# A stick-breaking triangle as two rounded products, a reordered seam and a later key rotation in a one-core transformer kernel

## The chip, the cores and the metric

The kernel runs on one core of a Trainium2 chip. The metric is the device time of one execution in microseconds (us). Engines are named as the profile names them: PE (TensorE matmul), PEld (TensorE weight load), DVE (VectorE), ACT (ScalarE), POOL (GpSimd) and SP (SyncE, which issues most DMAs).

## What is computed

One transformer block and then a second block of two layers, all in float32, on 256 tokens of width 1024. The part that the change touches most is the stick-breaking attention of the second block's token mixer (8 heads in each of the 2 layers), cut here to what matters:

```python
def stick_breaking_attention(q, k, v):
    ...
        z = jnp.einsum('bhqd,bhkd->bhqk', qc, k).astype(jnp.float32) * scale
        mask = kpos[None, :] < qpos[:, None]
        log_1m = jnp.where(mask, jax.nn.log_sigmoid(-z), 0.0)
        suffix = lax.cumsum(log_1m, axis=3, reverse=True) - log_1m
        w = jnp.where(mask, jnp.exp(jax.nn.log_sigmoid(z) + suffix), 0.0).astype(v.dtype)
        return jnp.einsum('bhqk,bhkd->bhqd', w, v)
```

The token mixer computes 8 heads of causal attention with rotary (moba), these 8 heads (sb) and 8 heads with latent queries and keys (mla), gates their projections and adds the result to x. The first block is built likewise (dilated and neighbourhood attention, then a gated feed-forward with a convolution over positions). Its residual sum has no norm on what is added (`x = x + gate1 * (merged @ w_out)`), while every residual sum of the second block norms it first (`x + res_w * (1 + gate) * rms_norm(y, g_post)`). All scales and shifts come from products of a condition vector with large "ada" matrices.

## The kernel before

**Matmuls.** Weights come in chunks of 128 x 2048 floats, 269 of them. SP loads a chunk into one of three raw buffers, ACT rounds it to float32r (`hi`, L922), DVE writes the remainder (`lo`, L1311, raw minus hi), and PE computes every large product as three float32r products: hi by hi, hi by lo, lo by hi (`three`, L517 to L520). Chunk c is split behind chunk c-3 or c-4, whose slot it takes. A few small products are plain float32: the attention scores (L802), the transposes, the weighted values (L852, L854) and the stick-breaking sums (L813 to L817). A plain float32 matmul is two MATMUL records in the profile.

**Order.** Every engine's instructions are written out by hand in program order, and semaphores join them. In a mixer, step s computes the chunk `slots[s]` on PE, and around it stand the pieces of attention of nearby heads. Heads 0 to 7 are moba (or dil), 8 to 15 are sb, 16 to 23 are mla. Chunks 8 to 15 of the slots are lat.0, lat.1, gate.0, gate.1, gate.2, then `uq`, gate.3 and `ukv` with one latent matrix each; their products are shorter (36 matmuls for uq, 18 for ukv, 48 for a gate).

**A stick-breaking head s** goes over the engines so: PE writes the scores into a PSUM bank (L802). ACT computes ln(1 + exp(-|z|)) into `work` (L1095 to L1099). DVE adds max(z, 0) (L1521, `softplus`) and masks the two diagonal squares (L1524), and raises `s_sp`. One step later PE waits for `s_sp` and adds three products of `work` with constant matrices to the bank (`turned`, L811 to L818): the triangle over the first 128 keys for all 256 queries (L813), ones (L815) and the triangle over the second 128 keys (L817). The chunk of that step stands behind them on PE. DVE then adds the mask (L1528, `log_weights`), and ACT takes exp (L1113).

**DVE in a mixer step**, in order (`mixing`, L1616): copies or merges of the chunk just computed, L1528 of the head before, L1311 of the coming chunk, L1521 and L1524 of this head, extras of the step, `o_second` (L1535), then one or two ada products (L1324, 128 x 1024 each, with their own three buffers and DMAs). The extras of step 12 are the latents: scaled by DVE (L1606), rounded by ACT (L1265), remainder by DVE (L1613), after which PE may start `uq`; and `rotate_mla_k` (L1585 to L1590), which is first read by the scores of head 16. Step 14 has `rotate_mla_q` (L1595 to L1600). At step 16 DVE copies the value parts of ukv out of PSUM (`take_v`, L1569), which frees the bank of gate.4.

**A seam** is where PE has finished a projection by rows (L695) and the next needs the new x: DVE multiplies each of the four PSUM banks by a gain row (`times`, L1438), adds it to x (`plus`, L1453), ACT sums squares and takes the root, x is scaled (`scaled_x`, L1461 and L1465; ACT L984), PE transposes it (L748), with some idle float32 products (`keep_busy`, L738) before and between, and ACT and DVE make `h_hi` and `h_lo`. `into_norm` (L1466) writes the DVE part. Of its un-normed uses only the one behind `o.out` (the tag "out") leads to a norm; the seam behind `o.down` is written out separately (L1741 on).

`ada_places` (L138) is the table that says behind which chunk each ada product stands on DVE; the order of SP's loads follows from it (a load of ada h waits for the use of ada h-3). `shift_and_gain` (L1333) turns finished ada columns into shifts and gains.

Of the kernel before, what the change touches and what calls it, by code (L numbers as in the profile page):

```python
# [12 lines left out]
P = 128  # L13
# [123 lines left out]

def ada_places():  # L138
    at = [-1] * ADA_START
    at += list(range(4, 21)) + [20, 20, 21, 22, 24, 25]  # L140
    at += [AT["o.out.0"] + 2 + i // 2 for i in range(3)]
    b = AT["o.up.0"]
    at += [b + 7 + 2 * i for i in range(6)]
    at += [AT["o.down.0"] + 2 + i for i in (0, 0, 1, 1, 2, 3, 3, 4, 4, 5, 6, 6, 7, 7, 8, FD - 1)]
    for l in range(LAYERS):
        b = AT[f"{l}.up0.0"]
        at += [b + 3 + i for i in range(20)] + [b + 24 + i for i in range(8)]
        s = AT[f"{l}.moba.k1"] + 2
        at += [s + i for i in range(2, 13)] + [s + i for i in range(16, 25)]
        g = AT[f"{l}.up2.0"]  # L150
        at += [g + 3 + i for i in range(8)]
        if l + 1 < LAYERS:
            at += [g + 11 + i for i in range(13)] + [g + 25 + i for i in range(3)]
    return at
# [46 lines left out]
def program(nc, d, known):  # L201

    with ExitStack() as ctx:
# [22 lines left out]
        con = sb("con", [P, NCCOL])  # L226
        dcon = sb("dcon", [P, NDCOL])
        cs = sb("cs", [P, D])
        mod = ada_out
        last_row = dcon[:, 0:D]  # L230
        gain = sb("gain", [P, 2 * 8 + LAYERS * 24])
# [15 lines left out]
        with ExitStack() as scope:  # L247
            sb("br_shift", [P, BR_SHIFT], F32, scope)
            ra = sb("ra", [P, 15, SEQ], F32, scope)
            rb = sb("rb", [P, 12, SEQ], F32, scope)  # L250
            br_hi = sb("br_hi", [P, 12, SEQ], F32R, scope)
            br_lo = sb("br_lo", [P, 12, SEQ], F32R, scope)
            gates_a = sb("gates_a", [P, 12, SEQ], F32, scope)
            with ExitStack() as inner:
                gates_b = sb("gates_b", [P, 8, SEQ], F32, inner)
            lat = sb("lat", [P, 4, SEQ], F32, scope)
            lat_sq = sb("lat_sq", [P, 3, SEQ], F32, scope)
            turn = sb("turn", [P, 2, SEQ], F32, scope)
            turn_qk = gates_a[:, 0:2, :]
            rs, lat_hi, lat_lo = turn, br_hi[:, 8:11, :], br_lo[:, 8:11, :]  # L260
# [253 lines left out]
        def _(eng):  # L514
# [291 lines left out]
            def turned(l, heads, s):  # L806
# [3 lines left out]
                if kind == "sb":  # L810
                    eng.wait_ge(*s_sp.at((l, s)))  # L811
                    bank = score_bank(heads, s)
                    mm(bank[:, 0:SEQ], dcon[:, DCOL["neg_tri"]], w[:, 0:SEQ], start=False, stop=False,  # L813
                       skip_group_check=True)
                    mm(bank[:, P:SEQ], dcon[:, DCOL["neg_ones"]], w[:, SEQ:TRI], start=False, stop=True,  # L815
                       skip_group_check=True)
                    ins = mm(bank[:, SEQ:TRI], dcon[:, DCOL["neg_tri"]], w[:, SEQ:TRI], start=False, stop=True,  # L817
                             skip_group_check=True)  # L818
                else:
                    eng.wait_ge(*s_normed.at((l, s)))  # L820
                    before = [i for i in range(s % 2, s, 2) if heads[i][0] != "sb"]
                    if before:
                        eng.wait_ge(*s_pt_copied.at((l, before[-1])))
                    if kind in ("moba", "mla"):
                        parts = [(0, 0), (P, P), (2 * P, 2 * P)]
                    else:
                        parts = [(u * SEQ + t * P, t * SEQ + u * P) for t in range(2) for u in range(2)]
                    for to, fro in parts:
                        ins = nc.tensor.transpose(turn_bank(s)[:, to:to + P], w[:, fro:fro + P], ident)
# [473 lines left out]
        def _(eng):  # L1303
# [164 lines left out]
            def into_norm(post, banks, pre, buf):  # L1468
# [4 lines left out]
                times(post, banks, buf, 0, 0)  # L1473
                plus(post, buf, 0, normed)
                times(post, banks, buf, 1, 1)
                if pre:
                    scaled_x(pre, buf, 0)
                times(post, banks, buf, 1, 0)
                plus(post, buf, 1, normed)
                if pre:  # L1480
                    half_of_x(pre)
                    scaled_x(pre, buf, 1)
# [34 lines left out]
            def softplus(l, heads, s):  # L1517
# [3 lines left out]
                stt(w[:, 0:TRI], score_bank(heads, s)[:, 0:TRI], 0.0, w[:, 0:TRI], ALU.max, ALU.add)  # L1521
                ve.drain()
                diagonal = two(w[:])[:, :, 0:P]
                tt(diagonal, diagonal, over(dcon[:, DCOL["sb_mul"]], 2), ALU.mult).then_inc(*s_sp.up((l, s)))  # L1524

            def log_weights(l, heads, s):
                eng.wait_ge(*s_turned.at((l, s)))
# [184 lines left out]
            for k in range(3):  # L1712
                if k < 2:
                    split_behind(f"o.out.{k}")
                ada(AT[f"o.out.{k}"])
            shift_and_gain("o.1", 24, par[:, PCOL["b_ada"]][:, 24:40], par[:, PCOL["g_ffn"]], gain[:, 8:16])
            into_norm("out", "o.out", "norm2", oa[:, 0:8, :])
            modulated("norm2", 8)
            split_behind("o.out.2")
# [36 lines left out]
            for l in map(str, range(LAYERS)):  # L1756
# [16 lines left out]
                split_behind(f"{l}.down0.10")  # L1773
                eng.wait_ge(*s_dcon_in.at("dcon"))
                eng.wait_ge(*s_causal_in.at("causal"))
                for i, name in enumerate(("q0", "k0", "v0")):
                    if i < 2:
                        rotate_moba(l, name)
# [1 line left out]
                    ada(AT[f"{l}.moba.{name}"])  # L1780
                mixing(l, MIX_HEADS, "moba.q1", MIX_SLOTS, {
                    0: [lambda: rotate_moba(l, "q1")], 2: [lambda: rotate_moba(l, "k1")], 8: [lambda: layer_post(l, 1)],
                    12: [lambda: latents(l), lambda: latents_second(l), lambda: rotate_mla_k(l)],
                    14: [lambda: rotate_mla_q(l)]})
                split(AT[f"{l}.out.3"])
                layer_gain(l, 2)
# [219 lines left out]
```

## Time and profile before

| what | value |
|---|---|
| median of 3 runs | 1710.9 us (1710.19 to 1712.64) |
| the profiled execution's own time | 1708.62 us |
| its span | 1706.8 us |
| PE busy | 1661.3 us, 97% |
| DVE busy | 1266.4 us, 74% |
| ACT busy | 872.6 us, 51% |
| mean granted TensorE clock | 0.997 |
| DMA | 398.80 MB, mean 234 GB/s |

The profile gives one execution. Busy time of PE is the union of its MATMUL records, which overlap since they are pipelined, so the durations of records add up to more than the busy time; what a matmul costs in a stream is read from the distance of the starts.

### The profile page before, as it was taken

To read this page: it belongs to the slowest core of one execution; us is meant where nothing else is said; L and a number is where in the kernel's file an instruction comes from. 1 tells how busy PE (TensorE), PEld (TensorE's weight loads), DVE (VectorE), ACT (ScalarE), POOL (GpSimd) and SP (SyncE) were. 2 spreads that over 40 slices of the span, in tenths; PEclk is the share of its full clock that TensorE was granted. 3 is DMA by queue.
4 is the path that set the end of the run, shared out by engine and by line. 5 is a ranking of instruction groups with operands and counts; after the bars stand their busy time and mean duration, and the time that the engine had idled before them with its cause. 6 is when DMAs were issued, how large, how long until landed. Compare 5 with 4: busy or idle time off the path is not lost.

```text
span 1706.8 us, 29606 instructions
## 1 busy us (share of the span) xinstructions
PE 1661.3 (97%) x12344; PEld 1551.4 (91%) x12344; DVE 1266.4 (74%) x1852; ACT 872.6 (51%) x1214; POOL 21.7 (1%) x39
## 2 busy tenths in 40 slices
PE   3999999999999999999999999999999999999998
PEld 3999889987999899989989998999899989989997
DVE  7777889977878677776878875877677776878553
ACT  4565466653543365675374344534355676373432
POOL 0000000000000000000000000000000000000000
PEclk9999999999999999999999999999999999999999
DMA  9878756777677745746548786687845746547552
GB/s 376 315 258 248 256 196 227 205 282 291 257 286 275 292 170 181 221 179 231 198 182 294 273 227 262 225 292 277 286 166 189 223 172 233 205 179 259 196 169 93
DMA packets 71078, 398.80 MB, mean 234 GB/s; under 512 B 8224, under 2 KB 8736, under 8 KB 36384
## 3 DMA queue, kind: packets, MB, share of 16 engines
q1 hardware_dynamic: 67968, 387.43, 64.3%
q0 software_dynamic: 2976, 9.47, 1.6%
q8 instruction: 98, 1.61, 0.4%
q14 instruction: 36, 0.29, 0.0%
HBM read 395.79 MB, written 1.08 MB: 233 GB/s over the span
## 4 chain that ended last, share of the span: by engine, by line
PE 76%; DVE 9%; ACT 6%; DMA 4%; DVEq 3%; issue 2%; SPq 1%; ACTq 0%
PE lin L518 17%; PE lin L520 17%; PE lin L519 17%; PE att L695 14%; DVE lo L1311 4%; ACT hi L922 3%; PE att L802 2%; PE lin L558 1%; DMA raw<-in_w 1%; PE lin L560 1%; PE lin L568 1%; DMA ada_w<-in_ada 1%; DVEq L1675 1%; DVE ada_w L1324 1%; ACT work L942 1%
## 5 line engine op out<-in xcount | busy, mean ns | idle before, releaser
L1311 DVE TENSOR_TENSOR lo<-raw,hi 128x2048 fp32r<-128x2048 f32 x269 | 615.4, 2291 | 251.8 <-ACT hi L922 251.5
L518 PE MATMUL lin<-h_hi,hi 128*128 128x256 f32 x2448 | 687.9, 281 | 1.1 <-DVE work L1670 0.7
L520 PE MATMUL lin<-h_hi,lo 128*128 128x256 f32 x2448 | 684.1, 279 | 0.0
L519 PE MATMUL lin<-h_lo,hi 128*128 128x256 f32 x2448 | 683.1, 279 | 0.0
L922 ACT ACTIVATE hi<-raw 128x2048 fp32r<-128x2048 f32 x269 | 513.3, 1911 | 193.2 <-PE att L695 118.3
L518 PEld LDWEIGHTS lin<-h_hi,hi 128*128 128x128 f32 x2448 | 460.4, 188 | 3.8 <-issue 3.7
L519 PEld LDWEIGHTS lin<-h_lo,hi 128*128 128x128 f32 x2448 | 460.5, 188 | 0.1
L520 PEld LDWEIGHTS lin<-h_hi,lo 128*128 128x128 f32 x2448 | 460.2, 188 | 0.0
L1324 DVE CUSTOM_DVE_ANT_0 ada_w<-ada_w,cs 128x1024 f32<-128x1024 f32 x179 | 217.6, 1218 | 18.5 <-DMA ada_w<-in_ada 18.4
L1162 ACT ACTIVATE work<-lin 128x256 f32<-128x256 f32 x88 | 33.8, 384 | 268.5 <-PE lin L520 267.5
L695 PE MATMUL att<-hi,act_hi 128*128 128x512 f32 x440 | 138.8, 389 | 0.0
L695 PE MATMUL att<-hi,act_lo 128*128 128x512 f32 x440 | 138.8, 389 | 0.0
L695 PE MATMUL att<-lo,act_hi 128*128 128x512 f32 x440 | 138.8, 389 | 0.0
L695 PEld LDWEIGHTS att<-lo,act_hi 128*128 128x128 f32 x440 | 82.6, 188 | 17.2
L695 PEld LDWEIGHTS att<-hi,act_lo 128*128 128x128 f32 x440 | 82.6, 188 | 17.2
L695 PEld LDWEIGHTS att<-hi,act_hi 128*128 128x128 f32 x440 | 82.2, 188 | 16.8
L518 PE MATMUL lin<-br_hi,hi 128*128 128x256 f32 x224 | 63.5, 283 | 0.1
L519 PE MATMUL lin<-br_lo,hi 128*128 128x256 f32 x224 | 62.6, 279 | 0.0
L520 PE MATMUL lin<-br_hi,lo 128*128 128x256 f32 x224 | 62.5, 279 | 0.0
L518 PE MATMUL lin<-hi,h_hi 128*128 128x256 f32 x192 | 54.3, 283 | 0.0
L558 PE MATMUL lin<-h_hi,hi 128*128 128x256 f32 x224 | 53.1, 282 | 1.1 <-ACT h_hi L1007 1.1
L520 PE MATMUL lin<-hi,h_lo 128*128 128x256 f32 x192 | 53.9, 281 | 0.0
(291 smaller groups left out, 2024.7 us busy)
## 6 DMA issues: line engine op xcount, KB each, us to landing
raw<-in_w SPq DMA_DIRECT2D x269, 1024.0 KB, 4.9
ada_w<-in_ada SPq DMA_DIRECT2D x179, 512.0 KB, 5.2
ada_s<-in_ada SPq DMA_DIRECT2D x13, 512.0 KB, 15.4
bias<-in_bias POOLq DMA_DIRECT2D x16, 256.0 KB, 4.3
ffn_row<-rows POOLq DMA_DIRECT2D x5, 512.0 KB, 9.2
x<-in_x SPq DMA_DIRECT2D x1, 1024.0 KB, 9.6
ra<-rows POOLq DMA_DIRECT2D x2, 512.0 KB, 5.0
dcon<-in_dcon SPq DMA_DIRECT2D x1, 896.0 KB, 7.6
```

Of the source, the lines that this page charges most:

```text
L518: mm(out, w_hi, a_hi, start=start, stop=False, skip_group_check=skip)
L519: mm(out, w_hi, a_lo, start=False, stop=False, skip_group_check=skip)
L520: return mm(out, w_lo, a_hi, start=False, stop=stop, skip_group_check=skip)
L558: mm(o, hi[SLOT[c]][:, b], h_hi[:, t, :], start=t == 0 and j == 0, stop=False, skip_group_check=True)
L560: mm(o, lo[SLOT[c]][:, b], h_hi[:, t, :], start=False, stop=False, skip_group_check=True)
L568: ins = mm(outs[i][:, j * SEQ:(j + 1) * SEQ], hi[SLOT[c]][:, b], h_lo[:, t, :], start=False, stop=t == 3, skip_group_check=True)
L695: ins = mm(att[:, 2 * a + n, :], act[:, t, tokens], w[s][:, kk * D + n * 512:kk * D + (n + 1) * 512], start=t == 0 and i == 0, stop=t == 2 ...
L802: ins = mm(out, q, k, start=start, stop=stop, skip_group_check=skip)
L922: act(hi[SLOT[c]][:], raw[:, c % RAW, :], ACT.Copy).then_inc(*s_hi.up(c))
L1162: act(work[2 + k % 2][:, 0:SEQ], lin[:, BANK[(c, 0)], 0:SEQ], ACT.Silu).then_inc(*s_gated.up((stage, k)))
L1311: tt(lo[SLOT[c]][:], raw[:, c % RAW, :], hi[SLOT[c]][:].bitcast(F32), ALU.subtract).then_inc(*s_lo.up(c))
L1324: ve.tensor_tensor_reduce(out=w, in0=w, in1=cs[:], scale=1.0, scalar=0.0, op0=ALU.mult, op1=ALU.add, accum_out=ada_out[:, h:h + 1]).then_i ...
```

## The change

1. The product of L813 (float32, 128 x 128 by 128 x 256) becomes two float32r products of the same size. DVE prepares their operands: a float32r copy `tri` of the triangle (once, in layer 0), and for each head a rounded copy `sp_hi` of the tile's first 256 columns and the remainder `sp_lo`; `s_sp` is raised by the latter. The two other products stay.
2. In `into_norm` without a norm, `scaled_x` of the first half of x stands behind `plus` of the second half.
3. `rotate_mla_k` stands in step 13 instead of 12.
4. Nine ada products of the first block's mixer and projection stand one or two chunks earlier, and some of those behind `o.down`; the shifts and gains of `o.1` are made behind `o.out.0`.

```diff
 def ada_places():
     at = [-1] * ADA_START
-    at += list(range(4, 21)) + [20, 20, 21, 22, 24, 25]
-    at += [AT["o.out.0"] + 2 + i // 2 for i in range(3)]
+    at += list(range(4, 21)) + [20, 20, 21, 22, 22, 23, 24, 25, 26]
     b = AT["o.up.0"]
     at += [b + 7 + 2 * i for i in range(6)]
-    at += [AT["o.down.0"] + 2 + i for i in (0, 0, 1, 1, 2, 3, 3, 4, 4, 5, 6, 6, 7, 7, 8, FD - 1)]
+    at += [AT["o.down.0"] + 2 + i for i in (0, 0, 1, 1, 2, 2, 3, 3, 4, 4, 5, 5, 6, 6, 7, FD - 1)]
...
+        tri = sb("tri", [P, P], F32R)
...
+            with ExitStack() as inner:
+                sb("under_sp", [P, 8, SEQ], F32, inner)
+                sp_hi = sb("sp_hi", [P, 2, SEQ], F32R, inner)
+                sp_lo = sb("sp_lo", [P, 2, SEQ], F32R, inner)
...
-                    mm(bank[:, 0:SEQ], dcon[:, DCOL["neg_tri"]], w[:, 0:SEQ], start=False, stop=False,
-                       skip_group_check=True)
+                    mm(bank[:, 0:SEQ], tri[:], sp_hi[:, s % 2, :], start=False, stop=False, skip_group_check=True)
+                    mm(bank[:, 0:SEQ], tri[:], sp_lo[:, s % 2, :], start=False, stop=False, skip_group_check=True)
...
-                if pre:
+                if pre and normed:
                     scaled_x(pre, buf, 0)
                 times(post, banks, buf, 1, 0)
                 plus(post, buf, 1, normed)
+                if pre and not normed:
+                    scaled_x(pre, buf, 0)
...
-                tt(diagonal, diagonal, over(dcon[:, DCOL["sb_mul"]], 2), ALU.mult).then_inc(*s_sp.up((l, s)))
+                tt(diagonal, diagonal, over(dcon[:, DCOL["sb_mul"]], 2), ALU.mult)
+                ve.drain()
+                ve.tensor_copy(sp_hi[:, s % 2, :], w[:, 0:SEQ])
+                ve.drain()
+                tt(sp_lo[:, s % 2, :], w[:, 0:SEQ], sp_hi[:, s % 2, :].bitcast(F32), ALU.subtract).then_inc(
+                    *s_sp.up((l, s)))
...
-            shift_and_gain("o.1", 24, par[:, PCOL["b_ada"]][:, 24:40], par[:, PCOL["g_ffn"]], gain[:, 8:16])
+                if k == 0:
+                    shift_and_gain("o.1", 24, par[:, PCOL["b_ada"]][:, 24:40], par[:, PCOL["g_ffn"]], gain[:, 8:16])
...
+                if l == "0":
+                    ve.tensor_copy(tri[:], dcon[:, DCOL["neg_tri"]])
...
-                    12: [lambda: latents(l), lambda: latents_second(l), lambda: rotate_mla_k(l)],
+                    12: [lambda: latents(l), lambda: latents_second(l)], 13: [lambda: rotate_mla_k(l)],
```

Two places of DVE's order matter below. Lines of the changed kernel are 4 to 14 higher than those before. The first is DVE in a mixer from head 12's softplus (`work<-att,work`) to the end of head 13's; `lat` are the latents, `turn` and `ra` belong to the key rotation. Before:

```order
L1521 SCALAR_TENSOR_TENSOR work<-att,work 128x384
L1524 TENSOR_TENSOR work<-work,dcon 128x2x128
L1606 SCALAR_TENSOR_TENSOR lat<-lat,lpar,turn 128x256 x3
L1613 TENSOR_TENSOR br_lo<-lat,br_hi 128x768
L1585 STREAM_SHUFFLE turn<-lat 128x256
L1587 TENSOR_TENSOR turn<-turn,dcon 128x256
L1588 TENSOR_TENSOR lat<-lat,dcon 128x256
L1590 TENSOR_TENSOR ra<-lat,turn 128x256
L1324 ISA ada_w,ada_out<-ada_w,cs 128x1024
```

and in the changed kernel:

```order
L1527 SCALAR_TENSOR_TENSOR work<-att,work 128x384
L1530 TENSOR_TENSOR work<-work,dcon 128x2x128
L1532 CAST sp_hi<-work 128x256
L1534 TENSOR_TENSOR sp_lo<-work,sp_hi 128x256
L1617 SCALAR_TENSOR_TENSOR lat<-lat,lpar,turn 128x256 x3
L1624 TENSOR_TENSOR br_lo<-lat,br_hi 128x768
L1328 ISA ada_w,ada_out<-ada_w,cs 128x1024
L1328 ISA ada_out 128x1
L1539 TENSOR_TENSOR work<-att,dcon 128x384
L1315 TENSOR_TENSOR lo<-raw,hi 128x2048
L1527 SCALAR_TENSOR_TENSOR work<-pt,work 128x384
L1530 TENSOR_TENSOR work<-work,dcon 128x2x128
```

Each head has the pair CAST and TENSOR_TENSOR behind it, and the four instructions of the rotation have gone from in front of the ada product; they now stand behind head 13's pair.

The second place is DVE at the seam behind `o.out`: the last split and ada products, the gains (`gain<-ada_out,par`), then the PSUM banks (`oa<-att,oa`). Before:

```order
L1311 TENSOR_TENSOR lo<-raw,hi 128x2048
L1324 ISA ada_w,ada_out<-ada_w,cs 128x1024
L1324 ISA ada_out 128x1
L1338 TENSOR_TENSOR ada_out<-ada_out,par 128x16
L1340 SCALAR_TENSOR_TENSOR gain<-ada_out,par 128x8
L1438 TENSOR_TENSOR oa<-att,oa 128x512 x2
L1453 TENSOR_TENSOR x<-x,oa 128x1024
L1438 TENSOR_TENSOR oa<-att,oa 128x512
L1461 TENSOR_SCALAR oa<-x,factor 128x1024
L1438 TENSOR_TENSOR oa<-att,oa 128x512
L1453 TENSOR_TENSOR x<-x,oa 128x512 x2
```

and in the changed kernel:

```order
L1328 ISA ada_w,ada_out<-ada_w,cs 128x1024
L1328 ISA ada_out 128x1
L1342 TENSOR_TENSOR ada_out<-ada_out,par 128x16
L1344 SCALAR_TENSOR_TENSOR gain<-ada_out,par 128x8
L1315 TENSOR_TENSOR lo<-raw,hi 128x2048
L1442 TENSOR_TENSOR oa<-att,oa 128x512 x2
L1457 TENSOR_TENSOR x<-x,oa 128x1024
L1442 TENSOR_TENSOR oa<-att,oa 128x512 x2
L1457 TENSOR_TENSOR x<-x,oa 128x512 x2
L1465 TENSOR_SCALAR oa<-x,factor 128x1024
```

No ada product stands behind the last split any more, and the scaling of the first half of x (`oa<-x,factor 128x1024`) has gone behind both halves' sums.

## Rows read from the trace of the kernel before

**Rows 1.** The page, busy time by engine.
```profile
PE 1661.3 (97%) x12344; PEld 1551.4 (91%) x12344; DVE 1266.4 (74%) x1852; ACT 872.6 (51%) x1214; POOL 21.7 (1%) x39
```

**Rows 2.** Waits: who waited for whom, total us, times, longest.
```profile
PE pt L813 <- DVE work L1524: 2.3, 2, 1.2
...
DVE work L1528 <- PE att L817: 13.5, 8, 3.3
```

**Rows 3.** Groups by form: busy us, mean ns, then idle before.
```profile
L1648 DVE TENSOR_TENSOR act_lo<-work,act_hi 128x256 fp32r<-128x256 f32 x88 | 37.4, 425 | 8.0 <-issue 1.7
...
L1646 DVE CAST act_hi<-work 128x256 fp32r<-128x256 f32 x88 | 25.9, 295 | 8.0
```

**Rows 4.** PE timeline, head 15's sums, then chunk gate.4: start, duration.
```profile
756.07 0.70 PE L813 MATMUL att<-work,dcon 128*128 128x256 f32 x2
756.61 0.38 PE L815 MATMUL att<-work,dcon 128*128 128x128 f32 x2
...
757.10 0.36 PE L518 MATMUL lin<-h_hi,hi 128*128 128x256 f32 x1
757.29 0.28 PE L519 MATMUL lin<-h_lo,hi 128*128 128x256 f32 x1
757.41 0.28 PE L520 MATMUL lin<-h_hi,lo 128*128 128x256 f32 x1
```

**Rows 5.** DVE timeline, heads 12 to 15 of layer 0: start, duration, [idle before].
```profile
732.69 0.42 DVE L1524 TENSOR_TENSOR work<-work,dcon 128x256 f32<-128x256 f32 x1 [0.43 <-issue]
...
736.09 0.44 DVE L1585 STREAM_SHUFFLE turn<-lat 128x256 f32<-128x256 f32 x1
...
737.79 1.22 DVE L1324 CUSTOM_DVE_ANT_0 ada_w<-ada_w,cs 128x1024 f32<-128x1024 f32 x1
...
742.23 0.42 DVE L1524 TENSOR_TENSOR work<-work,dcon 128x256 f32<-128x256 f32 x1
...
747.34 0.42 DVE L1524 TENSOR_TENSOR work<-work,dcon 128x256 f32<-128x256 f32 x1
...
751.37 0.56 DVE L1528 TENSOR_TENSOR work<-att,dcon 128x384 f32<-128x384 f32 x1 [0.61 <-PE att L817]
752.17 2.29 DVE L1311 TENSOR_TENSOR lo<-raw,hi 128x2048 fp32r<-128x2048 f32 x1 [0.24 <-ACT hi L922]
754.96 0.56 DVE L1521 SCALAR_TENSOR_TENSOR work<-att,work 128x384 f32<-128x384 f32 x1 [0.50 <-ACT work L1099]
755.59 0.42 DVE L1524 TENSOR_TENSOR work<-work,dcon 128x256 f32<-128x256 f32 x1
...
756.87 0.68 DVE L1569 COPY ra<-lin 128x512 f32<-128x512 f32 x1
```

**Rows 6.** ACT timeline, the rounding of the chunk that is split behind gate.2.
```profile
735.80 1.92 ACT L922 ACTIVATE hi<-raw 128x2048 fp32r<-128x2048 f32 x1
```

**Rows 7.** DVE timeline, seam behind o.out.
```profile
217.78 1.29 DVE L1438 TENSOR_TENSOR oa<-att,oa 128x512 f32<-128x512 f32 x2 [0.16 <-issue]
...
222.22 0.75 DVE L1461 TENSOR_SCALAR oa<-x,factor 128x1024 f32<-128x1024 f32 x1 [1.25 <-ACT factor L932]
...
223.64 1.29 DVE L1453 TENSOR_TENSOR x<-x,oa 128x512 f32<-128x512 f32 x2
```

**Rows 8.** PE timeline, seam behind o.out.
```profile
223.96 1.89 PE L738 MATMUL lin<-con 128*128 128x256 f32 x8
226.98 0.44 PE L748 MATMUL pt<-con,oa 128*128 128x128 f32 x2 [1.14 <-ACT oa L984]
```

**Rows 9.** DVE timeline, before the seam behind o.down.
```profile
407.85 1.23 DVE L1324 CUSTOM_DVE_ANT_0 ada_w<-ada_w,cs 128x1024 f32<-128x1024 f32 x1 [2.70 <-DMA ada_w<-in_ada]
...
412.35 1.28 DVE L1438 TENSOR_TENSOR flat_f<-att,ffn_row 128x512 f32<-128x512 f32 x2
```

**Rows 10.** Windows: us, PE, PEld, DVE, ACT, POOL busy, granted clock, DMA share, GB/s.
```profile
220.00:223.00 3.00, 0.88 (x5) 0.42 (x3) 1.75 (x4) 1.65 (x4) 0.00 (x0) 1.00 0.90 376
421.00:427.00 6.00, 5.60 (x17) 4.79 (x18) 2.88 (x8) 3.40 (x12) 0.00 (x0) 0.50 0.01 3
```

## Prediction

> **What bounds the kernel now.** I read the busy times first: PE is busy for 97% of the span and DVE for 74% [rows 1]. So work taken off PE shortens the kernel wherever nothing else is late, and work put on DVE costs only where PE waits for it. The waits say where that is, for the part that changes: PE waited for the masked softplus tile twice in the whole run (once in each layer), 1.2 us each, while DVE, which needs the sums of PE next, waited 13.5 us over eight heads [rows 2]. DVE is thus ahead of PE in most of the stick-breaking steps and behind it in a few. The timeline of DVE shows which: from head 12 to head 15 it has short waits only, 0.61, 0.24 and 0.50 us, all behind head 14 [rows 5]. There the chunks on PE are short (uq and ukv) and DVE has the latents and two rotations as extras. The rest of the change sits at the two seams of the first block, where PE idles; I read those from the timelines of DVE and PE.
>
> A difference of 0.2% (3.4 us) is about what a measurement of this kernel can tell from none.
>
> **Part 1, the triangle on PE.** From the start of the float32 product to that of the next one it is 756.61 - 756.07 = 0.54 us. A float32r product of the same 256 columns takes 0.12 us in a stream (757.41 - 757.29), and 0.19 us when it is the first behind float32 ones (757.29 - 757.10) [rows 4]. Two of them: 0.19 + 0.12 = 0.31 us, so 0.23 us less per head; I take 0.2, since a float32 product follows whose start may again cost a little. Bounds: 0 (the start behind another type eats it) and 0.3 (0.54 less two at 0.12). Were PE the bound at all 16 heads, this would be 3.2 us.
> The page "FP8 and Floating Point Precision" of the Trainium skill, section "TensorE Precision Notes", says that true FP32 makes four passes through the array. Four against two of 0.12 would be 0.24 less; the row of the trace has 0.54 for the four, start-up included.
>
> **Part 2, the pair on DVE.** CAST of 128 x 256 takes 295 ns and the subtraction 425 ns, the same shapes and types as in the feed-forward [rows 3]. Each is behind a drain; the gap that a drain leaves I read at head 15, where L1521 ends at 754.96 + 0.56 = 755.52 and L1524, behind a drain, starts at 755.59 [rows 5]: 0.07, I take 0.08. So `s_sp` comes 0.08 + 0.30 + 0.08 + 0.42 = 0.87 us later, and everything behind it on DVE 0.88 us later. 16 heads: 14 us of DVE work.
>
> For heads 8 to 12 that is covered by DVE's own waits for PE (13.5 us over eight heads), so these five keep the gain on PE. Before head 12's softplus three triangles count, so its chain, which hangs on PE, starts 0.6 us earlier: 732.09 instead of 732.69.
>
> From there I follow DVE [rows 5], T being the start of L1524 (or its successor):
> Head 13 was at 742.23, 9.54 behind head 12. The pair adds 0.88, the rotation that moves out takes away 737.79 - 736.09 = 1.70. DVE would then be ready for its split when ACT has rounded the chunk: that ended at 735.80 + 1.92 = 737.72 [rows 6] and moves with the latents by 0.88 - 0.6; the two meet, and I add 0.2 for ACT's logarithm, which was a little later. T13 = 732.09 + 9.54 + 0.88 - 1.70 + 0.2 = 741.0. The tile is ready 0.42 + 0.87 later, at 742.3, where the old one was at 742.65: the wait of 1.2 us becomes no longer.
> Head 14: 747.34 - 742.23 = 5.11, without a wait, plus the pair 0.88, plus the rotation 1.70 that now stands here. T14 = 748.7, 1.4 later than before; ready at 750.0. PE asks for it about then: head 13's sums from 742.4 (1.0 long, 757.10 - 756.07), 48 matmuls of gate.3 at 0.12, and under 1 us of value products, 750.1.
> Head 15: 755.59 - 747.34 = 8.25, plus 0.88, less the three waits, which get used up. They are 1.35 as labelled and 1.6 with the 0.09 by which two instructions in a row overlap. T15 = 756.2, ready at 757.5. Before, it was ready at 756.01 and PE began at 756.07. So PE begins 1.5 us later.
> Then the triangle saves its 0.2, but chunk gate.4 also needs the bank that L1569 frees: its second copy was at 756.87, the first 0.6 earlier, or 0.7 behind T15; with the pair and 0.68 for the copy that is 756.2 + 0.7 + 0.88 + 0.68 = 758.5. The chunk began at 757.10 [rows 4]: **1.4 us later, in each layer, 2.8 us in all**. This holds the gain of the earlier heads already. Bounds: -1.6 per layer (eight times 0.2, all of DVE's work hidden) and +3.0 (the waits of 1.6 stay, since what they wait for comes later too).
> A layer's seams, merges and DMAs behind this point are paced by PE, so I see nothing that gives it back.
>
> **Part 3, the seam behind o.out.** Of the ada products that stood in DVE's unbroken run from the last merges to the PSUM banks, one less stands there now: two leave at the end, one comes in ahead. One costs 1.22 us with 0.08 overlapped, 1.14. So the banks begin at 217.78 - 1.14 = 216.6 [rows 7]. The ada product that comes in also delays the merge that frees a PE bank: up to 0.6 us of wait on PE, which reaches the end only through the fourth bank. From 216.6 DVE has: two banks 1.29, the sum of the first half (twice 512 wide, as the two of 1.29 together) 1.3, two more banks 1.29, which end at 220.5; the sum of the second half 1.29, until 221.8, where it ended at 223.64 + 1.29 = 224.93; and then the scaling of the first half, at 221.8 instead of 222.22 [rows 7]. That is 0.4 earlier. PE began its idle products 223.96 - 222.22 = 1.74 behind the scaling's start; so now at 223.5, and they take 1.89, until 225.4. The second half's transposes waited until 226.98 for the scaled x [rows 8]; that is ready 3.1 us earlier now (224.93 against 221.8), so the idle products become the bound, and the transposes begin at 225.4. **1.6 us less.** Bounds: 1.1 (the ada product alone) and 2.6 (if the merge does not delay PE and the first half is ready at once).
>
> **Part 4, behind o.down.** DVE waited 2.70 us for an ada load there, and began with the banks at 412.35 [rows 9]. The loads are issued back to back, so moving uses earlier makes DVE wait for them earlier. After the last but one load there were one split, one ada product (4.5 us from 407.85 to 412.35); now an additional split stands behind it, and the load comes one chunk (some 2 us) earlier. I count +0.2, bounds -2 and +1.5. The copy of `tri`, once, and DMA order elsewhere: nothing; DVE has waits there.
>
> **Sum.** 2.8 - 1.6 + 0.2 = +1.4 us. On the profiled execution's own time, 1708.6, this gives 1710.0; the median of the runs is 2.3 us above it (1710.9), so I forecast **1712.3 us**, no difference that can be told.
>
> **Rivals.**
> *DVE's work is hidden everywhere.* For it: 26% of DVE is idle, and moving the rotation takes 1.70 us off head 13's path. Against: the waits between heads 12 and 15 sum to less than the added 3.5 us. Time: 16 x 0.2 = 3.2 and the seam's 1.6 less: 1710.9 - 4.8 = 1706.1, faster. Chance 0.16; a part of it (under 1 us per layer of delay) is in the forecast's own range.
> *The backlog is paid in full.* DVE is the bound from head 12 to the copies of ukv, the three waits stay, and each layer loses 3.0 us: 6.0 - 1.6 + 0.2 = +4.6, 1715.5, slower. It decides at head 14: if PE has to wait long for that tile too, nothing behind it can recover. For it: two rotations now lie between three heads in a row. Against: two of the three waits are for things (PE's sum, ACT's rounding) that do not need DVE first. Chance 0.15.
> *The clock falls.* In the seam behind o.down PE ran at a granted clock of 0.50 (1.2 GHz) from 421 to 427 us, after an idle time; in the one behind o.out it stood idle for over 2 of 3 us and kept 1.00 (2.4 GHz) [rows 10]. If the new idle time before head 15 did the former, each layer would lose half of such 6 us, 3 more: 1712.3 + 6 = 1718, slower. The page "TensorE: Matmul & The Clock Gate" of the Trainium skill, Part 1, says that a stretch of idleness throttles the array's clock. [...] Against: the new waits are no longer than the one that kept it. Chance 0.03.
> *The two products are no cheaper than the one.* That the change does not do on PE what it says: the start at each change of type eats 0.2 us. Then head 12 is not earlier, 0.6 per layer: 1713.5, no difference. Chance 0.06.
>
> **How the numbers follow.** The forecast has 0.60, the others as given; of the forecast's own spread 0.02 falls on either side of 0.2%. Faster by over 0.2% (under 1707.5) 0.18, slower (above 1714.3) 0.20, within 0.62. The range goes from 1706.5, just short of the end of the first rival, to 1715.8, which takes in the second.
>
> **What would show it.** In the changed kernel's profile: the pair in 0.8 to 0.9 us per head; head 12's and earlier sums on PE without a wait; waits of PE for `sp_lo` at heads 14 and 15 of both layers, some 0.3 and 1.9 us; gate.4 about 1.4 us later against head 12 than before, where head 15's tile waits on nothing but DVE. The second transposes at the seam behind o.out 1.6 us earlier against o.out's start, PE no longer idle between the two. I am wrong if PE waits for `sp_lo` nowhere, or if it waits at heads 8 to 11; or if the seam keeps its 226.98 - 223.96 between idle products and transposes.

## The result and the profile after

| | before | changed |
|---|---|---|
| median of 12 runs | 1708.33 us (1706.61 to 1712.64) | 1712.25 us (1708.63 to 1716.75) |
| ratio | | 1.0025, 95% interval 1.0017 to 1.0034 |
| span of the profiled execution | 1706.8 us | 1706.8 us |

The change makes the kernel slower by 0.25%: 4.3 us by the ratio, 3.9 us between the medians. The forecast time, 1712.3 us, was met to 0.1 us, but that is luck: its sum was +1.4 us where about +4 was measured, on a median of 1710.9 that came out 2.6 us lower with more runs, and the two errors cancel. What has to be explained is +4, not +1.4. The two profiled executions don't show it, since they have the same span (the changed kernel's is the fastest of its 12). So the stretches have to be compared one by one.

The page of the changed kernel, busy time by engine, which answers to [rows 1]:

```profile
PE 1659.5 (97%) x12344; PEld 1550.4 (91%) x12344; DVE 1278.3 (75%) x1885; ACT 873.9 (51%) x1214; POOL 21.8 (1%) x39
```

DVE has 12 us more work and PE 1.8 us less. The waits of PE for DVE that matter here, against one row of 2.3 us in [rows 2] (line, tile, whom it waited for: total us, times, longest). The first three are new; the last, for a merge, stands in the profile of before too, with 0.7 us:

```profile
PE att L817 <- DVE sp_lo L1534: 4.3, 4, 1.8
PE lin L522 <- DVE br_lo L1624: 1.9, 2, 0.9
PE pt L817 <- DVE sp_lo L1534: 1.1, 2, 0.6
PE lin L522 <- DVE oa L1562: 0.8, 1, 0.8
```

**The mixer.** DVE's timeline of layer 0, the mask, the cast and the subtraction of heads 12 to 15, beside [rows 5]:

```profile
727.36 0.42 DVE L1530 TENSOR_TENSOR work<-work,dcon 128x256 f32<-128x256 f32 x1
727.86 0.30 DVE L1532 CAST sp_hi<-work 128x256 fp32r<-128x256 f32 x1
728.23 0.43 DVE L1534 TENSOR_TENSOR sp_lo<-work,sp_hi 128x256 fp32r<-128x256 f32 x1
...
736.32 0.43 DVE L1530 TENSOR_TENSOR work<-work,dcon 128x256 f32<-128x256 f32 x1
...
744.00 0.42 DVE L1530 TENSOR_TENSOR work<-work,dcon 128x256 f32<-128x256 f32 x1
...
751.52 0.43 DVE L1530 TENSOR_TENSOR work<-work,dcon 128x256 f32<-128x256 f32 x1
```

The mask's starts are 8.96, 7.68 and 7.52 us apart. PE's timeline at the triangles of heads 13 to 15 and the start of gate.4, beside [rows 4]:

```profile
737.67 0.38 PE L817 MATMUL pt<-sp_hi,tri 128*128 128x256 f32 x1 [0.57 <-DVE sp_lo L1534]
...
745.35 0.39 PE L817 MATMUL att<-sp_hi,tri 128*128 128x256 f32 x1 [0.34 <-DVE sp_lo L1534]
...
752.87 0.58 PE L817 MATMUL att<-sp_hi,tri 128*128 128x256 f32 x1 [1.81 <-DVE sp_lo L1534]
753.25 0.42 PE L818 MATMUL att<-sp_lo,tri 128*128 128x256 f32 x1
...
754.17 0.56 PE L522 MATMUL lin<-h_hi,hi 128*128 128x256 f32 x1
754.53 0.41 PE L523 MATMUL lin<-h_lo,hi 128*128 128x256 f32 x1
754.74 0.41 PE L524 MATMUL lin<-h_hi,lo 128*128 128x256 f32 x1
```

Behind the wait of 1.81 us the float32r products stand 0.21 us apart (754.53 to 754.74), where they stood 0.12 apart in [rows 4]. The windows of that place show why; the granted clock stands behind the busy times of the five engines, as in [rows 10]:

```profile
752.00:753.00 1.00, 0.13 (x1) 0.13 (x1) 0.91 (x3) 0.39 (x1) 0.00 (x0) 0.79 0.43 123
753.00:754.00 1.00, 1.00 (x5) 1.00 (x6) 1.00 (x3) 0.00 (x0) 0.00 (x0) 0.50 0.98 418
754.00:755.00 1.00, 1.00 (x7) 1.00 (x7) 0.79 (x2) 0.00 (x0) 0.00 (x0) 0.50 1.04 442
755.00:756.00 1.00, 1.00 (x6) 1.00 (x6) 1.00 (x6) 0.30 (x1) 0.00 (x0) 0.50 0.09 33
756.00:757.00 1.00, 1.00 (x11) 1.00 (x10) 1.00 (x1) 1.00 (x5) 0.00 (x0) 1.00 0.00 0
```

PE starts again at a granted clock of 0.50 (1.2 GHz) and keeps it for three microseconds, with 5 to 7 products in each where there are 11 at 1.00. So the wait costs more than its own length. The other layer shows the same (0.50 from 1394.3 to 1397.7 us, behind a wait of 1.81).

**The seam behind o.out.** PE's timeline, first the wait ahead of it in the last chunk of the mixer, then the seam, beside [rows 8]:

```profile
185.69 0.36 PE L522 MATMUL lin<-obr_hi,hi 128*128 128x256 f32 x1 [0.80 <-DVE oa L1562]
...
218.78 2.32 PE L742 MATMUL lin<-con 128*128 128x256 f32 x10
221.76 0.44 PE L752 MATMUL pt<-con,oa 128*128 128x128 f32 x2 [0.66 <-DVE oa L1465]
...
222.69 1.89 PE L742 MATMUL lin<-con 128*128 128x256 f32 x8
224.42 0.38 PE L752 MATMUL pt<-con,oa 128*128 128x128 f32 x2
...
225.60 0.36 PE L562 MATMUL lin<-h_hi,hi 128*128 128x256 f32 x1 [0.15 <-ACT h_hi L1011]
```

From the idle products to the first chunk this seam takes 225.60 - 218.78 = 6.82 us. Before, it began at 218.56, the second transposes stood at 226.98 [rows 8] and the first chunk at 228.23: 9.67 us. DVE is why:

```profile
211.68 1.22 DVE L1328 CUSTOM_DVE_ANT_0 ada_w<-ada_w,cs 128x1024 f32<-128x1024 f32 x1
...
213.51 2.29 DVE L1315 TENSOR_TENSOR lo<-raw,hi 128x2048 fp32r<-128x2048 f32 x1
215.71 1.28 DVE L1442 TENSOR_TENSOR oa<-att,oa 128x512 f32<-128x512 f32 x2
...
220.96 0.75 DVE L1465 TENSOR_SCALAR oa<-x,factor 128x1024 f32<-128x1024 f32 x1
```

The banks begin at 215.71 instead of 217.78 [rows 7], which is 3.1 us ahead of PE's idle products instead of 0.8. The scaling begins 2.2 us behind the seam's start, where it was 3.7 behind.

**The stretches.** For the changed kernel and every experiment below I took the same distances on PE's timeline: a mixer from the first product behind its seam to the first idle product of the next seam, a seam from there to the first product behind it. A star marks a granted clock of 0.50 for some 3 us in the stretch (near 7 behind o.down in the kernel before and in e6). "e" numbers are the experiments.

| kernel | first mixer with o.out | seam behind o.out | seam behind o.down | mixer, layer 0 | mixer, layer 1 | ratio of its runs to before |
|---|---|---|---|---|---|---|
| before | 188.5 | 9.67 | 15.35* | 252.7 | 252.3 | 1 |
| changed | 188.9 | 6.82 | 13.76* | 255.0* | 255.3* | 1.0025 |
| e1 | 187.8 | 9.95* | 13.25* | 255.3* | 255.4* | 1.0029 |
| e2 | 187.7 | 9.98* | 13.18* | 255.9* | 254.0 | 1.0026 |
| e3 | 187.8 | 10.00* | 9.97 | 251.5 | 251.3 | 0.9987 |
| e4 | 188.8 | 6.83 | 11.99 | 252.7 | 252.3 | 0.9998 |
| e5 | 188.9 | 6.83 | 13.87* | 255.1* | 254.9* | 1.0034 |
| e6 | 188.9 | 6.82 | 15.99* | 253.9 | 253.8 | 1.0015 |
| e7 | 188.9 | 6.83 | 13.49* | 250.7 | 250.7 | 0.9975 |
| e8 | 189.3 | 6.85 | 13.19* | 251.5 | 251.1 | 0.9980 |
| e9 | 189.1 | 7.58 | 12.91* | 250.7 | 250.7 | 0.9975 |
| e10 | 189.2 | 7.58 | 12.01 | 251.4 | 251.7 | 0.9985 |
| e11 | 187.7 | 9.66 | 12.08 | 252.7 | 252.4 | 1.0012 |
| e12 | 187.7 | 10.61* | 9.74 | 252.7 | 252.3 | 1.0000 |

What a kernel leaves alone repeats to 0.1 us in the mixers (252.7 and 252.3 in four kernels), so one profile tells half a microsecond there, which the times alone do not. The seam behind o.down does not repeat, and nor do the feed-forwards (last section).

### The profile page after: what moved, and what is told of

It reads as the page before. It is cut to its first block, busy times and chain, and to the rows that moved or that the text cites. A ratio compares the mean times of both kernels' runs of the same rounds, so it can differ in the third digit from the quotient of the medians.

```text
span 1706.8 us, 29671 instructions
## 1 busy us (share of the span) xinstructions
PE 1659.5 (97%) x12344; PEld 1550.4 (91%) x12344; DVE 1278.3 (75%) x1885; ACT 873.9 (51%) x1214; POOL 21.8 (1%) x39
## 4 chain that ended last, share of the span: by engine, by line
PE 77%; DVE 9%; ACT 5%; DMA 4%; DVEq 3%; issue 1%; SPq 1%; ACTq 0%
PE lin L522 17%; PE lin L524 17%; PE lin L523 17%; PE att L699 15%; DVE lo L1315 4%; ACT hi L926 3%; PE att L806 2%; PE lin L562 1%; DMA raw<-in_w 1%; PE lin L564 1%; PE lin L572 1%; DMA ada_w<-in_ada 1%; DVEq L1686 1%; DMA ada_s<-in_ada 1%; PE att L856 1%
## 5 line engine op out<-in xcount | busy, mean ns | idle before, releaser
L1315 DVE TENSOR_TENSOR lo<-raw,hi 128x2048 fp32r<-128x2048 f32 x269 | 615.6, 2291 | 251.9 <-ACT hi L926 250.7
L1108 ACT ACTIVATE work<-work,mn 128x128 f32<-128x128 f32 (+1 forms) x96 | 44.4, 466 | 21.2 <-DVE mn L1501 21.2
```

Of the source, the lines that this page charges most:

```text
L1108: ins = act(w[:, cols], w[:, cols], ACT.Exp, bias=mn[:, s % 2, t:t + 1], scale=-1.0, accum_out=den[:, s % 2, t:t + 1])
L1315: tt(lo[SLOT[c]][:], raw[:, c % RAW, :], hi[SLOT[c]][:].bitcast(F32), ALU.subtract).then_inc(*s_lo.up(c))
```

## Experiments

All are timed in five rounds beside the kernel before on the same chip, whose median was 1704.12 us for e1 to e4, 1704.41 for e5 to e8 and 1705.41 for e9 to e12. The profile of the kernel before is from another execution on its own.

**e1: the pair with the later rotation alone.** The changed kernel without its parts 2 and 4: the old tables of ada products, the old place of the gains and of the scaling.

> Parts 1 and 3 alone (the pair and the later rotation); seams and ada products as before. My theory after reading the two traces: DVE's backlog makes PE start gate.4 1.4 to 1.5 us later in each layer, and the idle time before head 15 lets the granted clock fall for some 3 us, which costs 0.8 to 1.7 more; the whole change is 2.7 better than that because of the seam behind o.out. So this is slower than before by 2 x (1.45 + 1.2) = 5.3 us, between 3 and 7. Rival: the added time comes from the moved ada products or the seam (then this is within 1.5 us of before). Second rival, the clock drop is chance: 2.9 slower.

Measured: 1710.33 us, ratio 1.0029 (1.0017 to 1.0041), 4.9 us slower. The mixers are 2.6 and 3.1 us longer than in the profile of before, both with the clock at 0.50 for a while, and PE waits for `sp_lo` as in the changed kernel. That is the whole of the loss; the first rival falls, and the second (2.9 slower) lies just at the interval's lower end.

**e2: the pair alone, the rotation in step 12.**

```diff
-                    12: [lambda: latents(l), lambda: latents_second(l)], 13: [lambda: rotate_mla_k(l)],
+                    12: [lambda: latents(l), lambda: latents_second(l), lambda: rotate_mla_k(l)],
```

> Part 1 alone, the key rotation still in step 12. The rotation's 1.70 us then stands before head 13's softplus with the pair: PE's wait for head 13's tile grows from 1.2 to about 2.5 us, head 14's disappears, head 15's is 0.9 to 1.4. My theory: gate.4 2.0 to 2.3 us later per layer, so 4.3 slower by waits and 4 to 8 us slower in all, since the clock has two idle times to fall at. Rival: the rotation's place does not matter, because DVE's work up to head 15 is the same in sum: then the same as the kernel with both parts within 1 us.

Measured: 1709.89 us, ratio 1.0026 (1.0014 to 1.0037), the same as e1. PE's timeline at heads 13 and 15, first in layer 0, then in layer 1:

```profile
740.69 0.41 PE L818 MATMUL pt<-sp_hi,tri 128*128 128x256 f32 x1 [2.03 <-DVE sp_lo L1533]
...
756.15 0.38 PE L818 MATMUL att<-sp_hi,tri 128*128 128x256 f32 x1 [0.72 <-DVE sp_lo L1533]
...
1383.16 0.38 PE L818 MATMUL pt<-sp_hi,tri 128*128 128x256 f32 x1 [2.03 <-DVE sp_lo L1533]
```

Here the rival was right: the wait moves from head 15 to head 13 and its sum stays. Each layer has the same wait of 2.03 us, yet the clock fell behind it in layer 0 and held in layer 1, and the mixers are 3.2 and 1.7 us longer than before. That difference of 1.5 us is the clock's, within one execution.

**e3: the rotation in step 13 alone, one float32 product.** The diff of e2, upside down, on the kernel before.

> Part 3 alone: the key rotation a step later, the triangle still one float32 product. Head 13's tile comes 1.7 us earlier, so PE's wait of 1.2 us there goes, and head 14's is asked for 1.1 us after it is ready. My theory: what decides is DVE's start of head 15's tile, whose three short waits (1.35 us) shrink: 1.0 us faster per layer, 2.0 in all. Rival: the waits between heads 14 and 15 are for DVE's own order and stay, PE then waits at head 15 for what it won at head 13: no difference.

Measured: 1702.39 us, ratio 0.9987 (0.9977 to 0.9998), 2.2 us faster; mixers 1.2 and 1.0 us shorter, and no wait for `work` L1524 is left. So part 3 is a gain of its own: DVE had slack between heads 13 and 15 for exactly this rotation. The pair then used up that slack and more.

**e4: parts 2 and 4 alone**, the mixers of the second block as before.

> Parts 2 and 4 alone (scaling behind both halves' sums, ada products earlier); mixers as before. My theory: 2.6 us less at the seam behind o.out and 0.2 behind o.down, so 2.8 us faster, between 1.6 and 4. Rival: the gain in the profiled execution was the clock's phase and the true one is nearer the 1.6 that the order gives. Second rival: a later seam gives it back (no difference).

Measured: 1704.34 us, ratio 0.9998 (0.9988 to 1.0008). No difference, though the seam behind o.out takes 6.83 us, 2.8 less than before. The stretches say where it goes. The first mixer has 1.0 us more than in e3, all of it around a wait of PE for a merge (L1552, 0.8 us), which the ada product brought forward behind chunk 22 delays. The seam behind o.down takes 11.99 us, more than in e3 (9.97) and less than in e1 and e2 (13.2), so this profile doesn't settle whether the rest is lost there; e11 takes that up. The second rival was right in the time, though one of the two places lies ahead of the seam.

**e5: the changed kernel again.**

> The changed kernel itself, beside the next ones on the same chip. By the runs so far: 3.5 to 5.5 us slower than before. Its parts by my theory: mixers 2 x 2.6 with the clock's fall, the seam behind o.out 2.9 less, a merge in the first mixer 1.0 more, the seam behind o.down 0.4 to 2 more.

Measured: 1710.63 us, ratio 1.0034 (1.0022 to 1.0047).

**e6: four idle products in front of the wait for head 15's tile.**

```diff
                 if kind == "sb":
+                    if s == 15:
+                        keep_busy(4, nps)
                     eng.wait_ge(*s_sp.at((l, s)))
```

> The changed kernel with four idle float32 products (some 1.9 us) on PE, into a bank that nobody reads then, ahead of its wait for head 15's tile. They take the place of the idle time and change no wait. Theory of the clock: the granted clock stays at 1.00 behind head 15, gate.4 takes 5.8 us again instead of 6.6 to 7.2, and each layer is 0.8 to 1.7 us shorter than in the changed kernel: 1.6 to 3.4 us faster than that. Rival: the clock falls whether PE idles there or not (then the same time as the changed kernel, or 0.2 more for products that outlast the wait).

Measured: 1706.51 us, ratio 1.0015 (1.0007 to 1.0024), and no longer the changed kernel's 1.0034. PE's timeline behind head 15, then the granted clock there:

```profile
754.55 1.99 PE L742 MATMUL nps<-con 128*128 128x256 f32 x8
756.42 0.38 PE L819 MATMUL att<-sp_hi,tri 128*128 128x256 f32 x1
756.64 0.28 PE L820 MATMUL att<-sp_lo,tri 128*128 128x256 f32 x1
...
757.44 0.36 PE L522 MATMUL lin<-h_hi,hi 128*128 128x256 f32 x1
```

```profile
755.00:756.00 1.00, 1.00 (x7) 0.87 (x6) 0.78 (x3) 0.95 (x1) 0.00 (x0) 1.00 0.54 82
756.00:757.00 1.00, 1.00 (x8) 0.72 (x7) 1.00 (x3) 0.00 (x0) 0.00 (x0) 1.00 0.70 254
757.00:758.00 1.00, 0.92 (x9) 0.76 (x8) 1.00 (x3) 0.00 (x0) 0.00 (x0) 1.00 1.02 434
```

The clock stays at 1.00 and the mixers are 1.2 and 1.0 us shorter than in e5. The clock's share of the loss is shown: useless work on PE makes the kernel faster. What is left, 1.2 and 1.5 us over the kernel before, is the backlog itself. The medians are 4.1 us apart, more than the two mixers' 2.3; the rest I can't place (e5 has five runs). The profiled execution is e6's slowest (1711.71 us), with the longest seam behind o.down of all, so only its stretches are used here.

**e7: the pair for heads 8 to 11 only.**

```diff
-                    mm(bank[:, 0:SEQ], tri[:], sp_hi[:, s % 2, :], start=False, stop=False, skip_group_check=True)
-                    mm(bank[:, 0:SEQ], tri[:], sp_lo[:, s % 2, :], start=False, stop=False, skip_group_check=True)
+                    if s < PAIRED:
+                        mm(bank[:, 0:SEQ], tri[:], sp_hi[:, s % 2, :], start=False, stop=False, skip_group_check=True)
+                        mm(bank[:, 0:SEQ], tri[:], sp_lo[:, s % 2, :], start=False, stop=False, skip_group_check=True)
+                    else:
+                        mm(bank[:, 0:SEQ], dcon[:, DCOL["neg_tri"]], w[:, 0:SEQ], start=False, stop=False,
+                           skip_group_check=True)
```

with `PAIRED = 12`, and `softplus` raising `s_sp` behind the mask for the other heads.

> The changed kernel with the pair for heads 8 to 11 alone; heads 12 to 15 keep the one float32 product. Theory of the backlog: DVE's added work counts only behind head 12, so no wait is left at head 15, the clock holds, and the four early pairs are still covered and save 0.2 each on PE: mixers 1.1 (rotation) + 0.8 shorter than before, 3.8 in two layers; the seams add 0 to 1 more gain: 3 to 5 us faster than before, 8 faster than the changed kernel. Rival: the early heads' saving on PE is eaten because ACT or DVE paces those steps: then the gain is the rotation's 2.2 alone.

Measured: 1700.24 us, ratio 0.9975 (0.9965 to 0.9986): 4.3 us faster than before, and some 10 faster than e5. Mixers 250.7 twice, 2.0 and 1.6 shorter than before and 0.8 and 0.6 shorter than with the rotation alone (e3). That is the four early heads at 0.15 to 0.2 each. The rival falls.

**e8: no pair; rotation, seam behind o.out and a new table.** The second product of step 22 stands at 18, the places behind o.down as before.

```diff
-    at += list(range(4, 21)) + [20, 20, 21, 22, 22, 23, 24, 25, 26]
+    at += list(range(4, 19)) + [18, 19, 20, 20, 20, 21, 22, 23, 24, 25, 26]
```

> The parts that should help, alone: no pair, the rotation at step 13, the scaling behind both sums at the seam behind o.out with the ada products ahead of it, but the second product of step 22 at step 18 instead, and the places behind o.down as before. Theory: rotation 2.2 less, seam 2.9 less, no late merge in the first mixer, the seam behind o.down as before: 5 us faster than before (3.5 to 6). Rival: the ada load at step 18 comes late and makes DVE wait (then a wait of PE for a merge or a split in the first mixer, and 3 us faster only).

Measured: 1700.56 us, ratio 0.9980 (0.9971 to 0.9989), 3.4 us faster. The rival was right: the first mixer is the longest of all, 189.3, with two waits of PE for merges (0.5 and 0.6 us) instead of one of 0.8, and DVE waited 0.18 and 0.45 us for ada loads in the 8 us ahead of the first.

**e9: as e7, with the doubled product at step 24 and the old places behind o.down.**

```diff
-    at += list(range(4, 21)) + [20, 20, 21, 22, 22, 23, 24, 25, 26]
+    at += list(range(4, 21)) + [20, 20, 21, 22, 23, 24, 24, 25, 26]
```

> The pair for heads 8 to 11, the rotation at step 13, the scaling behind both sums with the ada products ahead of the seam behind o.out, but their second doubled step is 24 (under o.out.0, whose products take 7.3 us) instead of 22, and the places behind o.down as before. Theory: mixers 3.6 us less than before, the seam behind o.out 2.9 less, the merge wait of 0.8 in the first mixer gone, behind o.down as before: 6 to 7 us faster than before, 2 to 3 faster than the kernel with the pair to head 11 alone. Rival: the doubled product at step 24 makes the last splits late, so that the seam behind o.out keeps 1 us more: 5 us faster.

Measured: 1699.97 us, ratio 0.9975 (0.9965 to 0.9985), 4.3 us faster where 6 to 7 were expected, and the same as e7. A wait for a merge is still there (0.6, for another tile), the first mixer is no shorter (189.1), and the seam behind o.out keeps 0.75 us more, as the rival had it:

```profile
PE pt L753 <- DVE oa L1470: 1.4, 1, 1.4
PE lin L523 <- DVE ogates L1572: 0.6, 1, 0.6
```

**e10: as e9, with head 12 in two products as well** (`PAIRED = 13`).

> The same with head 12 in two products as well. The backlog theory counts DVE's added 0.88 us only from head 12's latents on, where 0.6 of it is won back by PE's earlier sums and the rotation has gone from ahead of head 13; a wait at head 15 of 0 to 0.5 us may appear. So 0.2 us less to 0.5 more per layer: within 1 us of the kernel to head 11. Rival: head 12 alone already pays its 0.88 in full, 1.8 us slower.

Measured: 1702.89 us, ratio 0.9985 (0.9975 to 0.9995), some 1.7 us slower than e9 by the ratios; mixers 0.65 and 1.07 longer. Its waits of PE have no row for `sp_lo`, but this one, which e9 has not:

```profile
PE lin L523 <- DVE br_lo L1632: 1.9, 2, 0.9
```

Head 12's pair stands in front of the latents on DVE, and uq on PE waits for their remainder. The rival's price was about right, at a place that neither theory had named.

**e11: only the ada products behind o.down a chunk earlier.**

> The kernel before with only the ada products behind o.down a chunk earlier. Theory from the traces: DVE has two splits and two products instead of one and two behind the last load it waits for, and begins with the banks 0.4 to 2.0 us later against PE's end of o.down; so 0.4 to 2 us slower, with the granted clock to add. The forecast had 0.2 slower. Rival: the load comes a chunk earlier and pays for the split: no difference.

Measured: 1707.23 us, ratio 1.0012 (1.0003 to 1.0022), 2 us slower. DVE's timeline ahead of the banks:

```profile
404.24 1.23 DVE L1324 CUSTOM_DVE_ANT_0 ada_w<-ada_w,cs 128x1024 f32<-128x1024 f32 x1 [0.41 <-DMA ada_w<-in_ada]
...
405.39 2.29 DVE L1311 TENSOR_TENSOR lo<-raw,hi 128x2048 fp32r<-128x2048 f32 x1
407.60 1.22 DVE L1324 CUSTOM_DVE_ANT_0 ada_w<-ada_w,cs 128x1024 f32<-128x1024 f32 x1
...
408.74 2.29 DVE L1311 TENSOR_TENSOR lo<-raw,hi 128x2048 fp32r<-128x2048 f32 x1
410.94 1.28 DVE L1438 TENSOR_TENSOR flat_f<-att,ffn_row 128x512 f32<-128x512 f32 x2
```

From the load waited for last to the banks it takes 410.94 - 404.24 = 6.70 us, against 4.50 with the old places [rows 9]. That load does not come so much earlier. Its ada product begins 9.1 us ahead of PE's idle products in the mean of the six profiles with the new places, and 7.9 us in that of the eight with the old ones. So the banks lead PE's idle products by 2.4 us instead of 3.4. Single profiles overlap (1.4 to 2.8 us against 2.2 to 4.9), and e11's own 2.55 lies above the 2.15 of the profile of before, so the direction rests on these means and on e11's runs.

**e12: only the scaling behind both sums.** The change's part 2 on the kernel before.

> The kernel before with only the scaling of the first half behind the second half's sum, at the seam behind o.out; ada products as before. By DVE's order: banks from 217.8, the second sum ends 1.25 earlier, the scaling starts 0.7 later, the idle products end at 226.6 where the second transposes began at 226.98: 0.4 us less. Theory: the ada products' places bring nearly all of the 2.9 us of that seam, the order of the scaling 0.4. Rival: the order alone gives 1.2 or more, since DVE's idle 1.25 us before the scaling goes.

Measured: 1704.55 us, ratio 1.0000 (0.9990 to 1.0011). The seam takes 10.61 us, 0.6 more than in e1 to e3 and 0.9 more than in the profile of before, where 0.4 less was expected. PE's timeline:

```profile
222.67 0.44 PE L748 MATMUL pt<-con,oa 128*128 128x128 f32 x2 [2.76 <-DVE oa L1461]
...
223.82 3.36 PE L738 MATMUL lin<-con 128*128 128x256 f32 x8
227.01 0.38 PE L748 MATMUL pt<-con,oa 128*128 128x128 f32 x2
```

Against e3 the scaling comes 0.6 us later, PE idles 2.76 us instead of 2.15, and the idle products then run at a granted clock of 0.50, as they do in e3 (3.36 us, where they took 1.89 at 1.00 [rows 8]). At the full clock they would have ended 1.5 us earlier, by that difference, and the seam would be shorter than before. So the order alone gives nothing. That it pays once DVE is free earlier is argued, not shown: no run has the new ada places without it.

## Why the prediction was right and wrong

**The pair.** Right. A head's pair takes 0.88 us with its drains (727.36 + 0.42 to 728.66), PE saves 0.2 per head, and head 12's and earlier triangles wait for nothing. e7 against e3 confirms the saving alone.

**The backlog from head 12 to head 15.** Right in kind, and nearly in size. The distances of DVE's masks were forecast as 8.9, 7.7 and 7.5 us and were 8.96, 7.68 and 7.52; waits at heads 14 and 15 as 0.3 and 1.9 us and were 0.34 and 1.81 (a third, 0.57 at head 13, I had called no longer than before). Gate.4 began 1.46 and 1.51 us later against the mixer's start than before; the term was 1.4. A part of the 1.46 is already the clock's: with the clock held (e6) gate.4 begins 1.17 and 1.51 us later, and the mixers are 1.2 and 1.5 us longer.

What I had not seen is that the gain of heads 8 to 12 is spent before: uq waits 0.9 us for the latents. I let it run into the term at head 12 (0.6 earlier) and got the right sum. e10 shows that wait by itself.

**The clock.** This is the first step that failed, and the largest: the forecast let the new waits keep the clock. I had its fall as a rival with a chance of 0.03, "the new waits are no longer than the one that kept it". But that one kept the clock in one execution only. In the profile of before PE idled 2.15 us at the seam behind o.out and stayed at 1.00 [rows 10]; in e3 it idled 2.15 us at the same place and fell. First the row of before, then e3's:

```profile
223.03 0.44 PE L748 MATMUL pt<-con,oa 128*128 128x128 f32 x2 [2.15 <-DVE oa L1461]
```

```profile
222.01 0.44 PE L748 MATMUL pt<-con,oa 128*128 128x128 f32 x2 [2.15 <-DVE oa L1461]
...
223.08 3.43 PE L738 MATMUL lin<-con 128*128 128x256 f32 x8
```

From 35 us on, where the records of the clock begin, it never fell behind waits of PE of 0.5 to 1.4 us. It fell in all eight mixers but one that had a wait of 1.8 to 2.0 us (changed kernel, e1, e2, e5), and at the seams it did either behind 2.05 to 2.90 us: nine waits of that length had it fall, five did not (the longest kept is the 2.90 of e11), and the four longer ones all had it fall. So a wait of 1.8 us costs 1.0 to 1.5 us more in nearly every layer, not with a chance of 3 in 100. It adds 2.3 us to the sum, where the rival had priced it at 6. The Trainium skill, "TensorE: Matmul & The Clock Gate", Part 1, says that the gate's phase runs on its own and that the same kernel meets it at another point from run to run; the two rows of 2.15 us fit that, though they don't prove it.

**The seam behind o.out.** The term -1.6 was mis-sized in two places that nearly cancel. The seam itself gave 2.85 us, more than the upper bound of 2.6: I counted one ada product less in DVE's run, yet the one that comes in stands where DVE has time, so both that leave count (2 x 1.14 us), and the banks began 2.3 us earlier against the seam's start, not 1.1. (By the two tables five ada products move ahead of this seam, not nine.) The product that comes in delays a merge, and this does reach PE: 1.0 us in the first mixer (e4 against e3), where I had put "up to 0.6" and let nearly all of it vanish. Net -1.85. The profile of before has such a wait too, by chance (0.73 us at 179.90; e1, e2, e3, e11 and e12 have none), which hid it further.

**Behind o.down.** The term +0.2 was too small. I had the load coming some 2 us earlier for a split of 2.2 us; by the means above it comes 1.2 us earlier. e11 shows 2 us slower (0.5 to 3.8 by its interval); over the profiles of the table the seam takes 12.4 us in the mean of eight with the old places and 13.5 in six with the new. The direction is shown by e11, the size only roughly: with the old places alone the banks' lead varies by 2.7 us from profile to profile, and the clock falls at this seam in nine of the fourteen.

**The sum, set right:** mixers 2.3 + 2.8 (the changed kernel and e5, in the mean, against before), seam behind o.out -2.9, merge +1.0 to 1.1, behind o.down +1.1: +4.3, against 4.3 by the ratio. The forecast's +1.4 lacked 2.3 us of clock and 0.9 behind o.down, and the seam behind o.out with its merge gave 0.25 more than forecast. The outcome lies just over the line of 0.2%, in the case "slower" that had 0.20, and inside the range. Of the rivals, the clock's had the right mechanism, though its price of 3 us a layer was over twice what was measured. "The backlog is paid in full" has the nearest sum, +4.6, but falls by e6: with the clock held a layer loses 1.2 to 1.5 us, not 3.0. "Hidden everywhere" and "two products no cheaper" fall by e1 and e7.

## What to carry to other kernels

Work moved from a full engine to one that is 74% busy is paid where the second has no waits of its own; so make the change head by head (or step by step) and keep it out of those steps: with the rest of the change in place, the pair in 8 of 16 places is 4.3 us faster than before, and in all 16 it is 4.3 slower. A new wait of PE near 2 us is to be priced with the clock behind it, and if the wait can't go, idle products into a free bank in front of it won 2.3 us in two layers here. A table of places should be changed one seam at a time, since a gain at one seam and the loss at the next are invisible in the sum, as in e4.

## What the runs showed of the hardware

The stretches of a feed-forward of the second block, from seam to seam, took either 183.2 or 184.3 us (the last one 189.25 or 190.35), never between: the longer one in 20 of the 56 stretches of these 14 profiles, in ten of them. The granted clock is 1.00 in both and PE has no idle time; the float32r products just come a little closer together or less close. The same 100 us of the same code in e3, then in e4 (busy time and number of instructions by engine, clock):

```profile
440.00:540.00 100.00, 100.00 (x859) 100.00 (x859) 81.56 (x109) 39.49 (x36) 0.00 (x0) 1.00 0.82 304
```

```profile
440.00:540.00 100.00, 100.00 (x852) 100.00 (x851) 80.47 (x109) 39.46 (x36) 0.00 (x0) 1.00 0.81 299
```

859 products against 852: 0.05 us in each chunk of 6.30 us, kept for a whole stretch. I have no cause for it. With four such stretches it makes 0 to 4 us of difference between two executions of one kernel, as much as the whole effect here, so single profiles are to be compared by stretch.
